# Second product of two squared-ReLU MLPs by a seven-product scheme on one Trainium2 core

## What is computed

```python
def squared_relu_mlp(x, w_up, w_down):
    return jnp.square(jax.nn.relu(x @ w_up)) @ w_down      # w_up 1024x4096, w_down 4096x1024

for i in range(2):
    mix = dsa_mixer(...) if i == 0 else gla_mixer(...)
    h = layer_norm(ALPHA * h + mix, ln_mix_g[i], ln_mix_b[i])
    h = layer_norm(ALPHA * h + squared_relu_mlp(h, mlp_w_up[i], mlp_w_down[i]), ln_mlp_g[i], ln_mlp_b[i])
```

## Time and profile before

| | us |
|---|---|
| three timed runs | 1858.11, 1860.78 (median), 1861.85 |
| profiled execution (its span; no other time of it is given) | 1860.1 |
| PE busy | 1826.0 (98%) |
| DVE busy | 1133.1 (61%) |
| ACT busy | 747.6 (40%) |
| POOL busy | 127.2 (7%) |

### The profile page before, as it was taken

How to read it: one execution, slowest core, us unless ns; L and a number is a source line. 1 busy time by engine, 2 the same in 40 slices (tenths; PEclk the granted TensorE clock), 3 DMA queues, 4 the chain that set the end, 5 groups by cost and what they waited for, 6 DMA issues and landing times.

```text
span 1860.1 us, 22821 instructions
## 1 busy us (share of the span) xinstructions
PE 1826.0 (98%) x9140; PEld 1489.7 (80%) x9140; DVE 1133.1 (61%) x1960; ACT 747.6 (40%) x1189; POOL 127.2 (7%) x124
## 2 busy tenths in 40 slices
PE   9999999999999999999999999999999999999998
PEld 7775787888888888878888888878756898888886
DVE  4987677555557578477744454787677643333338
ACT  4548342322233443554322322466466452222223
POOL 0341000000000054000000000000012000000001
PEclk9999999999999999999999999999999999999999
DMA  6221515444444122141443334222201413233221
GB/s 213 68 71 33 170 46 201 139 136 136 143 163 127 46 69 69 46 144 60 136 133 130 121 115 132 72 93 91 68 24 64 130 46 114 91 92 112 91 91 45
DMA packets 120330, 189.35 MB, mean 102 GB/s; under 512 B 7817, under 2 KB 72553, under 8 KB 117153
## 3 DMA queue, kind: packets, MB, share of 16 engines
q1 hardware_dynamic: 118688, 182.81, 29.9%
q0 software_dynamic: 1392, 4.82, 0.8%
q10 hardware_dynamic: 144, 0.26, 0.0%
HBM read 185.72 MB, written 2.16 MB: 101 GB/s over the span
## 4 chain that ended last, share of the span: by engine, by line
PE 81%; DVE 11%; ACT 5%; issue 2%; DMA 1%; POOL 0%; DVEq 0%; SPq 0%; ACTq 0%; POOLq 0%
PE bank L658 10%; PE bank L659 10%; PE bank L660 10%; PE bank L849 7%; PE bank L851 7%; PE bank L850 7%; PE bank L632 3%; PE bank L634 3%; PE bank L633 3%; PE bank L895 2%; PE bank L886 2%; PE bank L911 2%; DVE gb L2377 2%; DVE m L2375 1%; PE bank L760 1%
## 5 line engine op out<-in xcount | busy, mean ns | idle before, releaser
L2012 DVE TENSOR_TENSOR wl<-raw,wh 128x2048 fp32r<-128x2048 f32 (+1 forms) x137 | 307.9, 2252 | 192.5 <-ACT wh L1334 192.2
L1334 ACT ACTIVATE wh<-raw 128x2048 fp32r<-128x2048 f32 (+1 forms) x142 | 265.1, 1881 | 225.3 <-PE bank L851 89.1
L658 PE MATMUL bank<-xh,wh 128*128 128x512 f32 (+1 forms) x872 | 341.1, 391 | 1.0 <-DVE wl L2012 1.0
L659 PE MATMUL bank<-xh,wl 128*128 128x512 f32 (+1 forms) x872 | 340.3, 390 | 0.0
L660 PE MATMUL bank<-xl,wh 128*128 128x512 f32 (+1 forms) x872 | 340.1, 390 | 0.0
L849 PE MATMUL bank<-wh,uh 128*128 128x512 f32 x592 | 230.4, 389 | 0.7 <-DVE wl L2012 0.7
L850 PE MATMUL bank<-wl,uh 128*128 128x512 f32 x592 | 230.3, 389 | 0.0
L851 PE MATMUL bank<-wh,ul 128*128 128x512 f32 x592 | 230.3, 389 | 0.0
L658 PEld LDWEIGHTS bank<-xh,wh 128*128 128x128 f32 (+1 forms) x872 | 163.9, 188 | 38.5 <-issue 2.3
L660 PEld LDWEIGHTS bank<-xl,wh 128*128 128x128 f32 (+1 forms) x872 | 163.9, 188 | 34.7
L659 PEld LDWEIGHTS bank<-xh,wl 128*128 128x128 f32 (+1 forms) x872 | 163.9, 188 | 34.1
(11 more groups left out here) (375 smaller groups left out, 2957.5 us busy)
## 6 DMA issues: line engine op xcount, KB each, us to landing
raw<-in_mlp_w_up SPq DMA_DIRECT2D x32, 1024.0 KB, 5.9
raw<-in_mlp_w_down SPq DMA_DIRECT2D x32, 1024.0 KB, 5.1
raw<-in_w_ada SPq DMA_DIRECT2D x24, 1024.0 KB, 5.0
raw<-in_b_w_in SPq DMA_DIRECT2D x12, 1024.0 KB, 5.2
raw<-in_w_gate SPq DMA_DIRECT2D x11, 1024.0 KB, 5.3
raw<-in_w_up SPq DMA_DIRECT2D x11, 1024.0 KB, 5.4
raw<-in_w_in SPq DMA_DIRECT2D x10, 1024.0 KB, 5.1
raw<-in_w_down SPq DMA_DIRECT2D x10, 1024.0 KB, 5.0
```

What stands on the lines that cost most here:

```text
L658: pe.matmul(o, H[:, k, c], xh[:, k, :], start=k == 0, stop=False)
L659: pe.matmul(o, L[:, k, c], xh[:, k, :], start=False, stop=False)
L1334: act.activation(slots[slot_of[i]][0][:, 0:n], raw[:, i % NRAW, 0:n], ACT.Copy).then_inc(*s_high.up(i))
L2012: dve.tensor_tensor(L[:, 0:n], raw[:, i % NRAW, 0:n], H[:, 0:n].bitcast(F), ALU.subtract).then_inc(*s_low.up(i))
```

## The change

The second product of both MLPs is done, for n = 0..6, by Strassen's scheme in Winograd's form. The 512 hidden rows x 512 tokens and the 512 x 1024 weights are each cut into 2 x 2 blocks. Seven products of half size (256 tokens, 256 hidden rows, 512 columns: 2 x 2 x 3 = 12 matmuls each) replace eight. `down(7)` stays as it was.

For that, sums of blocks are needed on both sides. POOL makes four sums over weights in place in the raw buffers (`fold`, 128 x 1024 each) and four over squared hidden rows (`hidden_sums`, 128 x 2 x 256 each). The weights of one n become four parts: part 0 is chunk x as loaded, part 1 chunk x+1 with one half replaced, part 2 chunk x's buffer after two sums, part 3 a half chunk; each is split by ACT and DVE. The hidden rows are split seven times (once for each product) and no longer four. The affine pass goes from DVE to POOL, as soon as a pair of rows has been transposed.

```diff
+    def plan_fold(key, d, m, r0):
+        folds[key, d] = len(chunks)
+        slots(2, 0, 1, 3)
+        for c in range(2):
+            plan(m, r0, 4, c * 512, 512)
+        for nk in (4, 2):
+            slot_of[len(chunks)] = turn.pop(0)
+            chunks.append(([], nk, 512))
...
+        P1, P2, P6, P7, P5, P4, P3 = range(7)
+        OPERANDS = {P1: (0, 0), P2: (1, 0), P6: (1, 1), P7: (0, 0), P5: (0, 1), P4: (1, 1), P3: (1, 0)}
+        FACTORS = {P1: (0, 0), P2: (0, 2), P6: (2, 0), P7: (1, 0), P5: (3, 0), P4: (2, 2), P3: (1, 2)}
+        BEHIND = {P6: P1, P5: P6, P3: P5, P4: P7}
...
+            def fold(key, d):                      # PE
...
+                for s in range(7):
+                    part, k0 = FACTORS[s]
+                    H, L = parts(x + part)[0:2]
+                    w.wait_ge(*low_of(x + part))
+                    w.wait_ge(*s_xlow.at((key, "U", d, s)))
+                    for r in range(2):
...
+                        if s not in BEHIND:
+                            banks.take(name, s != P2)
+                            w.wait_ge(*banks.free(name, s_act.sem))
+                        else:
+                            w.wait_ge(*s_row.at((key, "Q", d, BEHIND[s], r)))
...
-                    down(key, n - 1, 4, False, look if n == 7 else 1)
+                    fold(key, n - 1)
...
+                for n in range(1, 8):              # DVE
...
+                    square(n, 0)
+                    square(n, 1)
+                    weights(x)
+                    square(n, 2)
+                    weights(x + 1)
+                    square(n, 3)
+                    weights(x + 2)
+                    cur.used = x + 4
+                    if n < 7:
+                        low_half_of(n, P4)
+                        added(d, P1)
+                        low_half_of(n, P1)
+                        weights(x + 3)
+                        added(d, P2)
+                        low_half_of(n, P2)
+                        added(d, P6)
+                        added(d, P7)
+                        low_half_of(n, P7)
+                        added(d, P5)
+                        weights(x + 4)
+                        low_half_of(n, P5)
+                        added(d, P4)
+                        low_half_of(n, P6)
+                        added(d, P3)
+                        low_half_of(n, P3)
...
+            def affine(x_key, n_gb):               # POOL
+                for t in range(T):
+                    w.wait_ge(s_gb, 16 * n_gb)
+                    w.wait_ge(*s_turn.at((x_key, t // 2, 3)))
+                    pool.tensor_tensor(h[:, t, :], h[:, t, :], gb[:, 0:D], ALU.mult).then_inc(*s_pool.up((x_key, "gain", t)))
+                    w.wait_ge(*s_pool.at((x_key, "gain", t)))
+                    pool.tensor_tensor(h[:, t, :], h[:, t, :], gb[:, D:2 * D], ALU.add).then_inc(*s_pool.up((x_key, "h", t)))
+
+            def fold(key, d):
...
+                w.wait_ge(*landed(x + 1))
+                pool.tensor_tensor(R0, R1, R0, ALU.subtract).then_inc(*s_pool.up(("fold", x, 1)))
+                w.wait_ge(*landed(x))
+                w.wait_ge(*low_of(x))
+                w.wait_ge(*s_pool.at(("fold", x, 1)))
+                pool.tensor_tensor(L0, L0, R0, ALU.add).then_inc(*s_pool.up(("fold", x, 0)))
+                w.wait_ge(*s_pool.at(("fold", x, 0)))
+                pool.tensor_tensor(L1, L1, L0, ALU.subtract).then_inc(*s_pool.up(("fold", x, 2)))
+                w.wait_ge(*low_of(x + 1))
+                pool.tensor_tensor(R0, R1, L0, ALU.subtract).then_inc(*s_pool.up(("fold", x, 3)))
+
+            def hidden_sums(key, n):
+                w.wait_ge(*s_step.at((key, "square", n, 1)))
+                w.wait_ge(*s_xlow.at((key, "U", n, P1)))
+                pool.tensor_tensor(quad(0, 0), quad(0, 0), quad(0, 1), ALU.subtract).then_inc(*s_pool.up((key, "S", n, P7)))
...
+            def mlp(key, x_key, n_gb):
+                affine(x_key, n_gb)
+                hidden_sums(key, 0)
+                for n in range(1, 8):
+                    fold(key, n - 1)
+                    if n < 7:
+                        hidden_sums(key, n)
```

More of the change, by code:

```diff
@@ L2208, in mlp, with low_half_of @@
[L2208 to L2227 removed]
+                def low_half_of(n, s):
+                    f, i = OPERANDS[s]
+                    u = place_of(n, s)
+                    w.wait_ge(*s_xhigh.at((key, "U", n, s)))
+                    dve.tensor_tensor(UL7[:, u], quad(f, i), UH7[:, u].bitcast(F), ALU.subtract).then_inc(*s_xlow.up((key, "U", n, s)))
@@ L3088, in sync_program @@
             fetch(2)
-            for i in range(NRAW, len(chunks)):
-                w.wait_ge(*low_of(i - NRAW))
+            for before, i in zip(fetched, fetched[NRAW:]):
+                w.wait_ge(*released(before))
+                if before in folds.values():
+                    w.wait_ge(*s_pool.at(("fold", before, 3)))
                 fetch(i)
```

260 lines of the change are left out of this document (191 added, 69 removed).

## The result

The changed kernel takes 1974.2 us (median of 4 runs, 1973.3 to 1975.3) against 1860.8 us for the kernel before on the same chip: 1.061 times the time, 95% interval 1.0595 to 1.0625. The direction was forecast, the size was not: 113 us more instead of 74, and 9 us above the range. The profiled execution took 1975.3 us, with a span of 1973.5.

What follows compares the result with a forecast made beforehand. PE was taken as the bound, busy 98% of the span. From 1860.8 us, -38.1 for matmuls, +54.6 and +25.9 for stalls, +28.6 crossings, +11 first steps (+82) gave 1943, less 8: 1935 us, own range 1910 to 1965 (8-in-10: 1878 to 1965).

Steps and rivals of the forecast that it cites:

- What bounds the kernel: Both MLPs' steps: PE is full, each matmul removed saves 0.2267 us; 14 downs with 84 matmuls for 96 save 38.1 us.
- The rule of turns: DVE and POOL operations that both read two SBUF operands exclude each other; the waiting one goes next, even for 2.4 us sums.
- The chain of m1: m1 step: DVE and POOL take turns preparing weights; third product starts at 13.2 for 5.4, stalling 7.8 us, seven times 54.6.
- The crossings: Entry to each MLP: POOL's affine operations delay DVE's root chain by 7.9 and later `xl` work by 6.4; 28.6 us for two.
- the root chain: Crossings, row 2's small DVE operations: 7.9 us later if each waits for POOL, 4.1 if only the `xl` operations wait.
- The first step: First step of each MLP: up(1,1)'s low half 3.8 us late, m1's first third product about 5 more; together 11 us.
- The 8 us taken off: Whole forecast: 8 us subtracted because unseen orders of waiting shorten rather than lengthen the chains, by up to 1.4 a step.
- the sum itself: Whole kernel: -38.1 + 54.6 + 25.9 + 28.6 + 11 = +82 us, giving 1943 before 8 us were taken off.
- The predicted sign: Steps, one down start to the next: 48 to 49 us in m1, 44 to 45 in m2, for 43.5, if right.
- No blocking that counts: Rival, all steps: POOL's long sums and DVE share SBUF, 0.7 us stall for each of 14; 1832 us, chance 0.12.
- Half as dear: Rival: POOL's waits slip into DVE's idle time or end after 1.3 us; stalls 40, crossings 21; 1884 us, chance 0.25.
- worse than 1965: Remaining case: DVE's 32 us plus POOL's 14.7 bound m1's step at 46.7 us and more; chance 0.05.

Runs made afterwards that it cites:

- e9_where_free: Kernel before with m1 unchanged; in m2 down products 1 to 6 as seven half-size products, weight sums on VectorE: 1849.2 us against 1860.6 (0.9933).
- e3_memset: Changed kernel with each of POOL's eight sums of a step replaced by two memsets of the same tile, output no longer the reference's: 1876.7 us.
- e1_affine_dve: Changed kernel with the affine pass back on VectorE, the rest as changed: 1954.0 us.
- e2_fill: Changed kernel with 28 (m1) or 12 (m2) useless matmuls for TensorE ahead of each fold's third product: 1953.0 us.
- e6_pauses: Kernel before, with TensorE made to wait for chains of GpSimd memsets in six down products of each MLP: 1922.8 us, 64 more than before.
- e4_sums_dve: Changed kernel with the four weight sums on VectorE, m1's second ada chunk and VectorE's first addition moved: 1896.5 us.
- e7_affine_first: Changed kernel with weight sums and affine pass both on VectorE, ada chunk and first addition moved: 1884.0 us.

## Why the prediction was wrong in size, step by step

- **What bounds the kernel** (PE full, each matmul taken out worth 0.227 us): right. e9_where_free gets 2.38 us for a fold; the forecast 2.72 was too high by 0.34. Of these, 0.31 lie at the third product (timeline of DVE and PE in the second fold):

```profile
992.00 1.28 DVE L2452 TENSOR_TENSOR h<-h,bank 128x512 f32<-128x512 f32 x2
...
992.83 0.47 PE L948 MATMUL bank<-wh,uh 128*128 128x512 f32 x1
```

The first of these two additions ends at 992.68, and the product goes on in its bank; at the pitch of 0.227 it would have started at 992.60. It starts 0.23 later, and the matmul behind it comes 0.08 late. So the same wait is left over, too short to be shown as a gap.
- **The rule of turns**, carried from operations of 0.6 to 1.3 us to sums of 2.4: right. The chain of m1 gave the third product at 13.2 us, measured 12.9; its stall 7.8, measured 7.1 (mean of the six later steps); m2 3.7, measured 3.4. e3_memset shows for the folds' forms that it is reading against reading, and for the greater part not GpSimd's time; its 0.74 us is the prediction's 0.7 without blocking, though with GpSimd operations a fifth shorter. What the rule lacks is the cast, which waits with one operand in SBUF.
- **The crossings**: the root chain at 7.9, the gap 7.56; the upper bound was the right one of the two, though not every operation waited: three did for a whole POOL operation. The second part at 6.4, gaps 5.4 and 4.7. e1_affine_dve shows the cause.
- **The first step**: 3.8 at up(1,1), measured 3.25; the extra stall of the first third product in m1 5, measured 3.1; m2 has one of 1.7 that the prediction put at nothing.
- **The 8 us taken off** for orders not seen: wrong. They were a guess in one direction, and nothing came of it.
- **The step that failed is the sum itself.** It priced each stall at its length and every matmul behind it at 0.2267 us, the pitch at full clock. "7 x 7.8" and "7 x 3.7" were lengths of gaps, not what they cost. 20 gaps of 2.9 to 10.2 us (two at each crossing, one in each up(1) and 14 in the folds) lowered the clock, and the matmuls behind them ran at half pace for a while: 41 us, over a third of the loss. The predicted sign shows it too: a step of m1 (343.08 to 393.67) lasts 50.6 us and not 48 to 49, with a gap that is no longer than forecast. The kernel before has no gap of this length near an MLP, so none of the rows chosen showed it; but the granted clock stands in every window, and the question "what does it do behind a gap" was not asked. e2_fill (same waits, full clock, 21 us less) and e6_pauses (gaps alone, 1.7 to 2.9 us behind each of 2.1 us or more, 2.1 on the mean) show it from both sides. With 20 x 2.1 = 42 added, and without the 8, the forecast would have been 1861 + 82 + 42 = 1985, for 1974. The 11 left are mostly the gaps, forecast 12.5 us too long in sum (120.1 for 107.6). In the recorded sum they hid part of the missing term, so the forecast came nearer than its terms deserve; that is luck.
- **The rivals.** "No blocking that counts" is out: the means of DVE's forms rose. "Half as dear" is out: the waits lasted whole POOL operations. Of "worse than 1965" the bound came true, but not its reason: a window from 343.08 to 393.67 has DVE busy 41.1 us of 50.6 with its waits for POOL counted in, and PE waited for the chain, not for DVE's sum of work.

The change as a whole fails because it puts 9.6 us of GpSimd's reads into a chain in which VectorE makes the same weights ready. With them on VectorE, and the ada chunk and one addition moved (e4_sums_dve), 78 of the 113 us are back, with the affine pass there too (e7_affine_first) 90. What the move to VectorE is worth without the new order wasn't run.

## What to carry to other kernels

Two-operand work given to GpSimd beside VectorE cost VectorE nothing here only where VectorE's second operand lay in PSUM, and memsets, which only write, cost nothing either. Everywhere else add the durations of both along the chain, count a tiny VectorE operation in the way as a whole GpSimd operation, and don't take a one-operand form (here a cast) to be safe. A gap of TensorE of a few us costs its length and here, from 2 to 3 us on, some 2 us more behind it, so by these prices many such stalls are dearer than one long one: read the granted clock behind every gap, and price it in a forecast. Before an operation is moved on its engine, ask what its end releases (a buffer, and the load that waits for it).

## What the runs showed of the hardware

- Operations on one or two columns wait as long as those on 2048: 2.3 us for 0.16 (root chain at the crossing).
- In the step of m1 shown above, where both engines have work ready, they alternate: neither gets two operations through while the other waits.
- A cast with one operand in SBUF (128x256, 0.29 us) lasted 2.46 us beside a GpSimd operation of 2.4 that reads two.
- Who waits shows it in different places: POOL's affine operations kept 2.40 us beside the root chain, where DVE's did the waiting; in the folds both lengthen (POOL's first sum 3.84 us).
- GpSimd's memset of 1024 columns takes 0.96 us, its sum of two operands 2.4; 0.53 and 1.3 for 512.
- The granted clock's fall costs about as much behind a gap of 2.1 us as behind one of 9.6 (1.9 and 2.5). Between 1.8 and 2.9 us it fell behind 10 gaps of 21, with equal gaps on either side; from 3.0 us on it fell behind each.
